# Differential attention on one core: the scores of three steps on stand between the transposes and the product with the values

## The reference

```python
def diff_attention(q1, q2, k1, k2, v, rel_bias, lam):
    ...
    def block(args):                       # 4 blocks of 128 queries
        i, q1b, q2b = args
        pos_q = i * Q_BLOCK + jnp.arange(Q_BLOCK, dtype=jnp.int32)
        mask = (pos_k[None, :] // CHUNK) <= (pos_q[:, None] // CHUNK)
        ...
        def probs(qb, k):
            s = jnp.einsum('bhqd,bhkd->bhqk', qb, k).astype(jnp.float32) * scale + bias
            return jax.nn.softmax(jnp.where(mask, s, -jnp.inf), axis=-1)

        w = probs(q1b, k1) - lam * probs(q2b, k2)
        return jnp.einsum('bhqk,bhkd->bhqd', w.astype(v.dtype), v)
```

## Time and profile before

| | |
|---|---|
| median of 3 runs | 1541.64 us (1540.03 to 1542.77) |
| profiled execution, its own time | 1542.75 us |
| its span in the trace | 1541.0 us |
| TensorE busy (PE in the profile) | 1443.9 us, 94% |
| VectorE busy (DVE) | 522.0 us, 34% |
| ScalarE busy (ACT) | 424.2 us, 28% |
| mean granted clock of TensorE | 0.981 |
| chain that ended last | PE 81%, DMA 11%, DVE 4%, ACT 2% |

### The profile page before, as it was taken

How to read it: one execution, slowest core, us unless ns; L and a number is a source line. 1 busy time by engine, 2 the same in 40 slices (tenths; PEclk the granted TensorE clock), 3 DMA queues, 4 the chain that set the end, 5 groups by cost and what they waited for, 6 DMA issues and landing times.

```text
span 1541.0 us, 16730 instructions
## 1 busy us (share of the span) xinstructions
PE 1443.9 (94%) x6940; PEld 910.3 (59%) x6940; DVE 522.0 (34%) x942; ACT 424.2 (28%) x732; POOL 32.1 (2%) x84
## 2 busy tenths in 40 slices
PE   6999998799999999998999879999999999999997
PEld 4777764485454445444454343555447888887885
DVE  4225546635211211121121045267344222223233
ACT  4125765513100000000200143156334222223222
POOL 0001110000000000000000011000000000000000
PEclk9999999899999999999999999999999999999998
DMA  9841127325799999999999751200004223222201
GB/s 335 286 168 55 55 83 309 128 100 229 298 427 428 428 427 427 425 397 405 389 377 415 290 195 55 71 40 1 0 0 175 99 109 110 85 79 110 82 0 55
DMA packets 30197, 313.88 MB, mean 204 GB/s; under 512 B 3908, under 2 KB 3908, under 8 KB 12456
## 3 DMA queue, kind: packets, MB, share of 16 engines
q1 hardware_dynamic: 22456, 295.54, 47.1%
q10 hardware_dynamic: 6512, 13.06, 2.6%
q0 software_dynamic: 1152, 4.19, 0.8%
HBM read 298.35 MB, written 14.43 MB: 203 GB/s over the span
## 4 chain that ended last, share of the span: by engine, by line
PE 81%; DMA 11%; DVE 4%; ACT 2%; issue 1%; SPq 0%; POOL 0%; ACTq 0%; DVEq 0%; POOLq 0%
PE ps L55 78%; DMA ring<-in_w 7%; DMA B<-in_w 2%; PE ps L1114 2%; DMA ring<-in_w_in 1%; PE ps L858 1%; DMA B<-yslots,SMI 0%; DVE X L1704 0%; ACT TMP L1373 0%; PE ps L606 0%; DVE TMP L1915 0%; DVE WL L1701 0%; PE ps L782 0%; ACT WH L1610 0%; PE ps L819 0%
## 5 line engine op out<-in xcount | busy, mean ns | idle before, releaser
L55 PE MATMUL ps<-ring,B 128*64 128x512 f32 (+2 forms) x880 | 263.7, 600 | 14.7 <-DMA ring<-in_w 13.1
L55 PEld LDWEIGHTS ps<-ring,B 128*64 128x64 f32 (+1 forms) x880 | 88.3, 147 | 135.9 <-issue 131.6
L55 PE MATMUL ps<-B 128*64 128x512 f32 (+5 forms) x440 | 148.4, 571 | 9.4 <-DMA ring<-in_w 6.6
L55 PE MATMUL ps<-XH,WH 128*128 128x512 f32 (+1 forms) x368 | 141.0, 383 | 1.3 <-DVE XL L1701 0.7
L55 PE MATMUL ps<-B,B 128*128 128x128 f32 (+1 forms) x1072 | 139.9, 291 | 0.4 <-DVE B L1970 0.4
L55 PE MATMUL ps<-XL,WH 128*128 128x512 f32 (+1 forms) x368 | 139.8, 380 | 0.0
L55 PE MATMUL ps<-XH,WL 128*128 128x512 f32 (+1 forms) x368 | 139.8, 380 | 0.0
L55 PEld LDWEIGHTS ps<-B,B 128*128 128x128 f32 (+1 forms) x1072 | 121.8, 190 | 25.8 <-issue 24.2
L1610 ACT ACTIVATE WH<-ring 128x2048 fp32r<-128x2048 f32 x33 | 63.2, 1916 | 167.9 <-PE ps L55 167.9
L1701 DVE TENSOR_TENSOR WL<-ring,WH 128x2048 fp32r<-128x2048 f32 x33 | 75.7, 2293 | 94.8 <-ACT WH L1610 94.8
L1441 ACT ACTIVATE TMP<-ps 64x512 f32<-64x512 f32 x32 | 19.0, 593 | 240.4 <-PE ps L55 240.4
(11 more groups left out here) (299 smaller groups left out, 1997.8 us busy)
## 6 DMA issues: line engine op xcount, KB each, us to landing
ring<-in_w SPq DMA_DIRECT2D x65, 2048.0 KB, 16.6
B<-in_w SPq DMA_DIRECT2D x24, 2048.0 KB, 17.3
ring<-in_w_ada SPq DMA_DIRECT2D x12, 2048.0 KB, 8.5
ring<-in_w_gu SPq DMA_DIRECT2D x11, 2048.0 KB, 8.3
ring<-in_w_in SPq DMA_DIRECT2D x7, 2048.0 KB, 12.5
TO<-in_w SPq DMA_DIRECT2D x7, 2048.0 KB, 16.6
ring<-in_w_down SPq DMA_DIRECT2D x5, 2048.0 KB, 7.3
yslots<-TMP ACTq DMA_DIRECT2D x64, 128.0 KB, 8.7
```

The costliest lines, as they stand in the source:

```text
L55: return e.matmul(o, l, r, start=first, stop=last, skip_group_check=True)
```

## The change

TensorE's loop is written in another order. Iteration 0 now issues the scores of steps 0 and 1, iteration 1 those of step 2, and each iteration i from 2 on issues the transposes of step i - 2, the scores of step i + 1, the product with the values of step i - 2, and then the modulation as before. The instructions and the semaphores that they wait for and raise are the same; VectorE, ScalarE, GpSimd and SyncE have the same streams.

```diff
+        def da_scores(i):
+            qt, h = DA[i]
+            w, p = 128 * qt + 128, 2 * (i % 2)
+            if i >= 2:
+                e.wait_ge(da_max, 2 * (i - 2) + 2)
+            for j in range(2):
+                m = mm(e, P[p + j][:, 0:w], dq[64 * j:64 * j + 64, h, 128 * qt:128 * qt + 128], dk[64 * j:64 * j + 64, h, 0:w], True, True)
+            m.then_inc(da_s, 1)
+
         for i in range(18):
-            if i < 16:
-                qt, h = DA[i]
-                w, p = 128 * qt + 128, 2 * (i % 2)
-                if i >= 2:
-                    e.wait_ge(da_max, 2 * (i - 2) + 2)
-                for j in range(2):
-                    m = mm(e, P[p + j][:, 0:w], dq[64 * j:64 * j + 64, h, 128 * qt:128 * qt + 128], dk[64 * j:64 * j + 64, h, 0:w], True, True)
-                m.then_inc(da_s, 1)
-            if i >= 2:
+            if i == 0:
+                da_scores(0)
+                da_scores(1)
+            elif i == 1:
+                da_scores(2)
+            else:
                 qt, h = DA[i - 2]
                 b = 6 + qt % 2
                 if i >= 3:
...
                 for c in range(qt + 1):
                     t = e.transpose(P[4][:, 128 * c:128 * c + 128], E[(i - 2) % 3][0][:, 128 * c:128 * c + 128], ident)
                 t.then_inc(da_T, 1)
+                if i + 1 < 16:
+                    da_scores(i + 1)
                 if i == 2:
                     e.wait_ge(sb_oT, 4)
```

## The result

The changed kernel takes 1532.07 us (median of 5 runs, 1529.23 to 1533.82) against 1541.05 us for the kernel before in the same runs: a ratio of 0.9939, 95% interval 0.9925 to 0.9954, that is 9.4 us less (7.1 to 11.6). The forecast was 1533.5 us, 8.1 us less. Measured once more in other runs the ratio was 0.9940 (0.9914 to 0.9966).

What follows compares the result with a forecast made beforehand. No engine was full; hand-overs between engines set the pace. Gains 2.1 + 7.7 less 1.6 make 8.2, called 8.1: 1542.75 profiled becomes 1534.6, and the median, 1.1 lower, 1533.5 us; 8-in-10 range 1530.3 to 1537.5.

Steps and rivals of the forecast that it cites:

- all behind it moves along: Behind the loop: TensorE's chain sets when the experts' loads begin, so time won in the loop moves everything behind it.
- swallow the gain: Rival, experts' stage: an earlier TensorE only waits longer for DMA; no change, 1541.6 us, chance 0.04.
- (a): Loop's opening: VectorE's copy of the modulation's row is hidden, so the first turn no longer waits; 2.1 us gained.
- (b): TensorE's regular stop between transposes and product, steps 3 to 13: the moved scores fill it; 7.7 us gained.
- (d): Steps 6, 8, 10, 12: VectorE and ScalarE not ready for an earlier TensorE; 0.4 us each, 1.6 us taken back.
- (c): Last steps, from step 12: the chain runs over VectorE and ScalarE, so the scores of steps 14 and 15 gain nothing.
- (e): Scores now ahead of product and modulation: they do not have to wait, so the change adds no waits.
- (f): TensorE's clock in the stage: both spells at 1.2 GHz stay as they are, so no gain or loss.
- The hand-over chain: Rival: ScalarE and VectorE set the pace from the transposes of step 6 on; gain 5.3 us, 1536.3 us, chance 0.17.
- The clock stays up: Rival: the low-clock spell at 271.5 does not come or the later ends sooner; gain 10 us, 1531.5, chance 0.12.
- The slower cases: Rival: TensorE falls to 1.2 GHz for far more of the stage; 1554 if half its busy time, chance 0.03.
- The signs: Changed kernel's profile: copy waits about 6 us, no first-turn wait, last product with the values near 295.5 us.

Runs made afterwards that it cites:

- Before, rows first: The kernel before, with VectorE's copy of the modulation's row ahead of the bias pass in odd iterations; ratio to the kernel before 0.9981.
- fill only: Against the changed kernel, the scores between transposes and product are those of step i, without the added step of look-ahead; ratio to the kernel before 1.0009.
- ScalarE later: The changed kernel with three small pieces of ScalarE's own work (a square, a row norm, a copy) one iteration later; ratio to the kernel before 0.9932.
- Scores twice: The changed kernel with each score pair computed twice into the same banks; ratio to the kernel before 0.9965, median 1534.63 us.
- product too: The changed kernel with the modulation's product of iterations 2 to 10 also ahead of the product with the values; 1525.72 us, ratio to the kernel before 0.9902.
- ahead only: Scores issued as early as in the changed kernel, but ahead of the transposes, so nothing stands between transposes and product; ratio to the kernel before 0.9982.
- Projection fills: The kernel of product too, with the first piece of the output projection put into the loop's last steps; ratio to the kernel before 0.9929.
- changed again: The changed kernel, nothing altered, measured and profiled once more beside other runs; ratio to the kernel before 0.9940.
- fill, rows first: The kernel of fill only, with VectorE's copy of the modulation's row ahead of the bias pass in odd iterations; ratio to the kernel before 1.0005.

## Why the prediction was right, point by point

**That the loop is where it happens, and that all behind it moves along: right.** The loads behind the first used-up expert block start 10.6 us earlier. From the first transposes of X to the end it is 1190.4 us before and 1191.2 us in the changed kernel. The other kernels have 1184.5 to 1191.4 us there, with no clear relation to their loop. The experts' DMA did not swallow the gain. The parts below add up to 9.8 us of the loop (2.4 + 6.8 + 0.6), less 0.8 in the output projection, where the forecast had 8.1: each part came out a little larger than forecast, and the clock, which was counted as nothing, took some of it back.

**(a) The opening, 2.1 us: right.** From the first scores to the first transposes it was 8.56 us and is 6.18, 2.4 us. The 0.3 us above the forecast are pitches: two score pairs behind each other took 1.91 us instead of 2 x 1.06, and the norm ahead of the transposes 0.86 instead of 0.95. *Before, rows first* won 1.6 of it by VectorE's order alone: it was indeed the copy behind the bias pass.

**(b) and (d), the filled stops less what is taken back, 7.7 - 1.6 = 6.1 us: right in sum.** From the first transposes to those of step 12 it was 51.8 us (241.87 to 293.70) and is 45.0 (237.86 to 282.88), 6.8 us. What I gave as the reason for (b), that the narrower scores fit the stop, is true but only half: *fill only* fills the same stops and wins nothing. The sentence in (d) that the moved scores help VectorE too is the other half, and I had priced it at nothing. The size of (d), taken as what is missing from the 7.7 of (b), was somewhat too large: 0.9 us in place of 1.6. Its mechanism is shown for two of its four places: in steps 6 and 8 the stops were 3.4 us together and are 3.2 with 1.3 us of scores put into them, so 1.0 us came back; *ScalarE later* took 1.5 us of these stops away by ScalarE's order alone. At steps 10 and 12 the forecast counted the same 0.4 us each. Step 10 has 0.4 us of stop left where it had 0.5; at step 12 it is the new wait of 0.5 us for the combination.

**(c) The last steps, nothing: 0.6 us.** From the transposes of step 12 to the end of the loop it was 11.1 us and is 10.5. *Scores twice* and *product too* have 10.5 us there as well, *ahead only* 9.7. *Projection fills* shows that the row behind this end waits for VectorE and ScalarE.

**(e) No new waits: right** but for 0.5 us for the combination in step 12.

**(f) The clock: right** in that both spells stayed, and the granted clock of the loop is 0.92 as before. The first was 3.43 us for the product instead of 3.08, a little longer. The second, counted from the end of the loop, lasted 1.7 us longer than before, and that in the dense matmuls of the projection: this is the 0.8 us between loop and X. In *changed again* it ended earlier and that loss was not there, so this part of the time is chance.

**The rivals.** The hand-over chain does take over, but only from step 12 on; ahead of it only the stops of steps 6, 8, 10 and 11 are left. *The clock stays up* was a real possibility one step away: in *scores twice*, *product too*, *ScalarE later*, *before, rows first* and both orders that only fill the first spell, the one behind step 6 or 8, is absent. The slower cases did not come near.

**The signs** that it named came out: TensorE's waits for the copy fell to 6.9 us (forecast about 6), the first turn has no wait, the last product with the values starts at 292.06 us (forecast 295.5; 1.6 us of the difference is the earlier start), and in the first half of the loop no wait for the combination or the exponentials appeared.

## What to carry to other kernels

A stop of the busiest engine is worth filling only with work whose user has time: here scores put into the stop gave nothing while VectorE waited for them, and 9.8 us of the loop once they were issued one step earlier, which by itself gave 3.8. Before moving a filler, look at what it covers where it is now: the piece of the projection taken forward left 3.5 us open behind it, and the low clock after that stop cost another 1.6. The best version found, with the modulation's product in the stop too, is 15 us faster than the kernel before.

## What the runs showed of the hardware

In this loop, in which TensorE is busy 77% of the time before and 85% in the changed kernel, its granted clock fell in some orders of the same work and not in others. In the changed kernel it went to 1.2 GHz after a stop of 2.07 us in step 8 (windows above: 0.59 on average for 4 us), in *ahead only* after one of 1.91 us (the product behind it took 2.86 us), and stayed at 2.4 GHz with stops of 1.55 and 1.64 us in *ScalarE later* and *scores twice*. The length of the stop alone does not decide it: in the kernel before it fell after 1.53 us and not after 1.91, in *before, rows first* it fell neither after 1.56 nor after 1.92, and in *fill, rows first* not even after 2.29:

```profile
276.02 0.68 PE L55 MATMUL ps<-B,TMP 128*128 128x128 f32 x4 [2.29 <-ACT TMP L1380]
276.63 1.92 PE L55 MATMUL ps<-ring,MISC 128*32 128x512 f32 x16
```

A spell behind step 6 or 8 cost 0.9 to 1.5 us in the modulation's product alone (2.86 to 3.43 us instead of 1.92).

Single executions of one kernel differed by up to 12 us (1532.7 to 1544.6 for the kernel before over one set of runs). In the traces the start of the loop lies between 230.1 and 233.5 us and the stretch from the transposes of X to the end between 1184.5 and 1191.4, while the loop of the two kernels that were profiled twice repeated to 0.2 us or better. A change of 3 us is better read from the length of its stage in the trace than from a few times, and *fill, rows first* warns that one trace isn't enough for that either.
